# The squares of the second part's three norms summed on GpSimd, with one product with ones in place of eight

## The reference, cut to what matters

```python
def rmsnorm(x, gain):
    y = x * lax.rsqrt(jnp.mean(x * x, axis=-1, keepdims=True) + EPS)
    return y * gain

for i in range(2):
    h = rmsnorm(x, norm_mix[i])
    mix = s5_mixer(h, ...) if i % 2 == 0 else dsa_mixer(h, ...)
    x = x + mix
    x = x + swiglu(rmsnorm(x, norm_ffn[i]), w_gate_up[i], w_down[i])
```

## Time and profile before

| what | us |
|---|---|
| median of three executions | 3164.7 |
| the profiled execution, its own time | 3160.65 |
| its span, from first to last instruction | 3158.8 |
| busy: TensorE products | 2900.4 (92%) |
| busy: VectorE | 1864.0 (59%) |
| busy: ScalarE | 1393.9 (44%) |
| busy: GpSimd | 219.7 (7%), 167 instructions |

### The profile page before, as it was taken

The page is one execution under the profiler, slowest core; times in us unless marked ns, Lnnn a source line. Parts: engine busy times, 40 slices in busy tenths (PEclk is TensorE's granted clock), DMA queues, the critical chain, the costliest instruction groups (busy, mean ns, idle before and its releaser), DMA issues.

```text
span 3158.8 us, 35772 instructions
## 1 busy us (share of the span) xinstructions
PE 2900.4 (92%) x12800; PEld 2235.7 (71%) x12800; DVE 1864.0 (59%) x2206; ACT 1393.9 (44%) x1794; POOL 219.7 (7%) x167
## 2 busy tenths in 40 slices
PE   7999999985899999999993678999989999989998
PEld 2548878765677777777772566788867767768887
DVE  3435653564988888888887753333236685343322
ACT  2323233223667777777775323323223435333221
POOL 1100100003930000000001000000001100000000
PEclk9999999996999999999997879999999999999999
DMA  6921722314899989999993802222221110122221
GB/s 236 330 76 60 282 85 94 121 62 161 319 331 352 387 351 387 361 377 369 369 372 108 107 32 75 94 95 106 93 75 67 67 54 1 41 72 101 94 94 67
DMA packets 90801, 546.92 MB, mean 173 GB/s; under 512 B 9232, under 2 KB 18848, under 8 KB 32384
## 3 DMA queue, kind: packets, MB, share of 16 engines
q1 hardware_dynamic: 79584, 485.65, 41.6%
q0 software_dynamic: 10816, 59.58, 5.5%
q10 hardware_dynamic: 288, 0.15, 0.0%
HBM read 516.51 MB, written 41.42 MB: 177 GB/s over the span
## 4 chain that ended last, share of the span: by engine, by line
PE 69%; DVE 17%; issue 6%; DMA 4%; ACT 3%; SPq 1%; POOL 1%; DVEq 0%; ACTq 0%; PEldq 0%; POOLq 0%
PE bank L348 38%; PE bank L286 6%; PE bank L1138 5%; PE bank L1142 4%; PE bank L1141 4%; DVE expert_low L2218 4%; DMA arena<-in_we_stream 2%; ACT expert_high L1587 1%; PE bank L1370 1%; PE bank L1392 1%; PE bank L1383 1%; DMA arena<-in_mod 1%; PE bank L1122 1%; DVE expert_x_low L2303 1%; DVE arena L2320 1%
## 5 line engine op out<-in xcount | busy, mean ns | idle before, releaser
L2218 DVE TENSOR_TENSOR expert_low<-arena,expert_high 128x2048 fp32r<-128x2048 f32 x291 | 684.2, 2382 | 102.7 <-ACT expert_high L1587 85.4
L1587 ACT ACTIVATE expert_high<-arena 128x1024 fp32r<-128x1024 f32 x582 | 597.2, 1057 | 213.4 <-PE bank L1138 117.5
L348 PE MATMUL bank<-high_b,weight_parts 128*128 128x512 f32 x1872 | 592.9, 398 | 29.6 <-DVE low_b L2456 15.9
L716 DVE TENSOR_TENSOR weight_parts<-ring_pages,weight_parts 128x1024 fp32r<-128x1024 f32 x185 | 226.7, 1226 | 557.9 <-ACT weight_parts L708 557.4
L708 ACT ACTIVATE weight_parts<-ring_pages 128x1024 fp32r<-128x1024 f32 x185 | 196.1, 1060 | 591.6 <-PE bank L348 552.4
L348 PEld LDWEIGHTS bank<-high_b,weight_parts 128*128 128x128 f32 x1872 | 352.8, 190 | 121.1 <-issue 36.3
L348 PE MATMUL bank<-low_b,weight_parts 128*128 128x512 f32 x832 | 325.7, 391 | 0.0
L1138 PE MATMUL bank<-expert_high,expert_x_low 128*128 128x512 f32 x768 | 309.5, 403 | 14.1 <-DVE expert_low L2218 10.4
L1141 PE MATMUL bank<-expert_high,expert_x_high 128*128 128x512 f32 x768 | 301.1, 392 | 0.0
L1142 PE MATMUL bank<-expert_low,expert_x_high 128*128 128x512 f32 x768 | 300.6, 391 | 0.0
L348 PE MATMUL bank<-hidden_parts,weight_parts 128*128 128x512 f32 x1056 | 240.0, 389 | 4.3 <-DVE hidden_parts L2502 4.3
(11 more groups left out here) (464 smaller groups left out, 4033.2 us busy)
## 6 DMA issues: line engine op xcount, KB each, us to landing
arena<-in_we_stream SPq DMA_DIRECT2D x294, 1024.0 KB, 6.5
ring_pages<-in_wb_stream SPq DMA_DIRECT2D x93, 1024.0 KB, 4.8
ring_pages<-in_wa_stream SPq DMA_DIRECT2D x49, 1024.0 KB, 4.9
arena<-in_mod POOLq DMA_DIRECT2D x16, 1024.0 KB
xbuf<-arena POOLq DMA_DIRECT2D x25, 512.0 KB, 15.9
arena<-xbuf SPq DMA_DIRECT2D x17, 512.0 KB, 7.3
ybuf<-arena SPq DMA_DIRECT2D x16, 512.0 KB, 2.6
arena<-kd SPq DMA_DIRECT2D x8, 512.0 KB, 24.1
```

Source lines behind the costliest of these rows:

```text
L348: ins = pe.matmul(o, lhsT, rhs, start=start, stop=stop)
L716: nc.vector.tensor_tensor(low, src, high.bitcast(F32), ALU.subtract).then_inc(weights_split, 1)
L1587: nc.scalar.activation(ehigh[c % HIGH_E][:, at], ring_e[c % RING_E][:, at], ACT.Copy) \
L2218: nc.vector.tensor_tensor(elow[c % RING_E][:], ring_e[c % RING_E], ehigh[c % HIGH_E][:].bitcast(F32), ALU.subtract).then_inc(weights_split ...
```

## The change

GpSimd adds the eight squares of each norm into the first tile, with seven additions of 128x512 in place, each waiting for its square and for the addition before. It raises `sq_summed` by a separate instruction. TensorE waits for that one increment (the two of the first block make it count from 2) and multiplies the one summed tile by the ones. The sums of norms 2 and 3 stand in GpSimd's program behind the stores of the state-space matrices and ahead of the wait and the loads of the rotary tables. The sum of norm 4 stands behind the loop of the rotated tiles. Nothing else is changed.

```diff
@@ -909,6 +909,14 @@
+            def squares_summed(n):
+                for kt in range(1, KT):
+                    pool.wait_ge(S["b_sq_full"], KT * (n - 2) + kt + 1)
+                    link(nc.gpsimd.tensor_tensor(sqb[n][:, 0, :], sqb[n][:, 0, :], sqb[n][:, kt, :], ALU.add))
+                pool.sem_inc(S["sq_summed"], 1)
+
+            squares_summed(2)
+            squares_summed(3)
             pool.wait_ge(S["b_x_ready"], 2 * KT)
             for dst, src in ((cossin, io["cossin"]), (rope, io["rope"]), (half1, io["half1"])):
                 pool.dma_start(dst, src).then_inc(S["b_rope_in"], 16)
@@ -926,6 +934,7 @@
+            squares_summed(4)
         @block.tensor
@@ -1189,10 +1198,8 @@
             def squares(n):
                 ps = opened(f"sn{n}")
-                for kt in range(KT):
-                    pe.wait_ge(S["b_sq_full"], KT * (n - 2) + kt + 1)
-                    ins = pe.matmul(ps[:], ones[:], sqb[n][:, kt, :], start=(kt == 0), stop=(kt == KT - 1))
-                ins.then_inc(bank_done, 1)
+                pe.wait_ge(S["sq_summed"], n + 1)
+                pe.matmul(ps[:], ones[:], sqb[n][:, 0, :], start=True, stop=True).then_inc(bank_done, 1)
```

## The result

Over eleven executions of each, side by side on one chip, the changed kernel has a median of 3255.05 us (3172.36 to 3259.99) and the kernel before one of 3244.42 us (3161.42 to 3256.53). Taken on its lower end that is 11 us of loss, in the middle 17 us; I had forecast 9.5 us of loss and a time of 3171 us.

The account below looks back on a forecast made before the run. TensorE was taken to bound the kernel, waiting at the norms for the three roots. Roots later by 5.3, 2.1 and 2.1 us, together 9.5, on 3160.65 gave 3170.2; forecast 3171 us, range 3163 to 3183.

Parts of the forecast that it names:

- a median that lands on such a one: Whole kernel: the measured median falls on a disturbed execution like the one at 3247.57 us; chance 0.01.
- Squares in a burst, adding slower than squaring: Before each norm: squares start 0.52 us apart over about 5 us, GpSimd additions take 1.30 us each.
- Seven additions: GpSimd at each norm: seven chained additions of 1.30 us with 0.08 us between two, 9.58 us.
- The overlap with VectorE's last addition at norm 2: Norm 2: first GpSimd addition meets VectorE's last addition to x for 0.3 us, costing 0.0 to 0.5, taken as 0.
- Release by a separate increment: Each norm, GpSimd's last addition to TensorE: 0.29 us, ends 0.1 and 0.4.
- The product at the lower clock: TensorE's one product at each norm, after a gap above 6.56 us: 2.08 us, against 1.02 at full clock.
- The sum for a norm: First square's start to root's start: 13.20 us, roots 5.3, 2.1 and 2.1 us later at norms 2, 3, 4.
- What was costed at nothing: Later rotary table loads (cover 4 us), the low clock behind norms, ScalarE's table load, and VectorE overlap: 0 us.
- The ends of the range: Lower: full clock, shorter addition, plain release, 3164.7 us; upper: wider addition, overlaps, slower releases, the median's 4 us, 3182.9.
- additions keep up: Rival at the norms: additions keep pace with squares, only the last shows; norm 3 gains 2.8 us, total 3154; chance 0.04.
- The rival of a low clock: TensorE's clock stays low behind the norms' longer gaps, up to +220 us in an up projection, 3390; chance 0.01.
- The mutual hindrance of GpSimd and VectorE: Rival at the norms: additions take 3.36 us throughout, 43 us more, 3213; chance 0.02.

Follow-up runs that it names:

- early_sums: Changed kernel with a longer filler ahead of attention and ScalarE's squares of tiles 0 to 6 moved into the stage before; 3188.39 us, ratio 1.0077.
- experiment 5: Changed kernel with a longer filler ahead of attention, TensorE making 44 or 24 small products while waiting for the sum; 3201.88 us, one execution.
- after_again: Changed kernel timed once more with no edit and no added filler; 3178.26 us, ratio 1.0055.
- fill2_after: Changed kernel with longer filler ahead of the attention steps and more filler products further on in that stage; 3175.65 us, ratio 1.0045.
- fill2_before: Kernel before with longer filler ahead of the attention steps and more filler products further on in that stage; 3168.08 us, ratio 1.0018.

## Why the prediction was right or wrong

**The time was wrong.** The step that failed is the one in which I set 3247.57 aside as a disturbed execution and gave 0.01 to a median that lands on such a one. About half of the kernel's executions are at that level: the attention stage has two lengths by TensorE's clock, and what TensorE does in a wait of 1.52 us just ahead of it decides whether it takes the long one (with a longer filler there the highest cluster was empty in both kernels). The sum was put on 3160.65, an execution that had kept its clock; the measured median, 3255.05, is one that had not. Why the clock falls there in one execution and holds in the next is open. I had looked for what the clock does behind the norms and nowhere else; the profile before had happened to hold its clock, so nothing in it showed the cost, and only the three times did.

**The mechanism was right, and its size to 1 us** (8.6 of holes against 9.5). By its terms:

- Squares in a burst, adding slower than squaring: shown. Spreading them (early_sums) moved the holes from 31.1 to 16.5 us in all.
- Seven additions, 9.58 us forecast, 9.46, 9.37 and 9.38 measured: 1.26 us each, not 1.30, with pitches of 1.34. The scaled width (1.24) was the nearer row. The overlap with VectorE's last addition at norm 2, costed at 0.0 to 0.5, was 0.16: the first addition took 1.42.
- Release by a separate increment: 0.29 forecast, 0.19 us at norm 3 (2352.15 to 2352.34).
- The product at the lower clock: 2.08 forecast, 2.05 measured, 1.12 when TensorE was kept at work (experiment 5).
- The sum for a norm: 13.20 forecast, 12.97 at norm 2, 12.88 at norm 4 (2859.85 to 2872.73).
- What was costed at nothing held at the norms: the tables had landed in time, and root to next product stayed at 6.52 us, clock or no clock.
- The ends of the range: the terms gave 3164.7 at the lower one, and the range began at 3163 without a term for the rest; the wider addition is 3 x 0.78 = 2.3, not 2.5. Neither matters beside the 85 us.

**The loss measured as a ratio is larger than the holes:** 17 us against 8.6. Part of it is the executions between the clusters, of which the one profiled had its clock fall at the second place; without the two of the first eleven, the three left are 8 us above the median of the four lowest of before (3173.4 and 3165.3). With the clock held in both kernels it is 7.6 us. By the counts the change makes such a fall more likely (5 of the 15 that were not in the highest cluster, against 0 of 39); why it should, with stages that start 5 to 10 us later and the same instructions, is open. A further 1.6 us came behind a wait of 2.17 us between the up and the down projection, which both kernels have. Here the profile after, then that before:

```profile
2180.00:2260.00 80.00, 77.83 (x336) 63.90 (x336) 24.45 (x25) 19.95 (x23) 0.00 (x0) 0.98 0.26 92
```

```profile
2180.00:2260.00 80.00, 77.83 (x344) 64.13 (x343) 23.99 (x24) 18.83 (x21) 0.00 (x0) 1.00 0.26 92
```

Root 2 to root 3 is 383.65 us against 380.23, 1.6 more than the hole (383.64 in after_again). The second feed-forward block does the same: from root 4 to the end it is 383.5 us in both profiles of the changed kernel and 381.9 in that before. From norm 2 on, with the attention stage left out, the changed kernel is thus 8.6 + 1.6 + 1.5 = 11.7 us longer in these profiles, as much as lies between the lowest clusters (by how much the part ahead of norm 2 differs changes from profile to profile). These falls come and go and are not the change's alone: fill2_after has neither (382.08, the hole's 1.83 and no more, and 381.9), fill2_before has the second (383.5). What decides them is open.

**The rivals.** That additions keep up did not happen; with the squares spread it nearly does, and the 2.8 us at norm 3 that it promised became 1.8. The rival of a low clock had the right engine and the wrong place: not behind the norms, where it came back within the first groups, but in the stage of short products. The mutual hindrance of GpSimd and VectorE is there beside dense work (1.74 us) and absent in the holes, where VectorE is idle.

## What to carry to other kernels

Moving work off the bounding engine gains nothing where its consumers wait for the mover: compare the pace of the producer (0.52 us a square) with that of the new engine (1.34 us an addition), and look first whether the producer could be spread, since early squares with a two-step sum gained back the 8.6 us of holes that the change had lost, and 12.7 us more. When the few times of a kernel scatter by 3%, find out where before you forecast: a second profile of the slow kind showed it in one row of slices. In this kernel a stage of short products kept TensorE busy and at half clock for 100 us, and a few filler products ahead of it and in it moved the median of the executions more than any edit of the norms. Those ahead of it alone did only half the work: 17 of 19 executions then lay where a later fall in the stage puts them.

## What the runs showed of the hardware that was not expected

- TensorE stayed at PEclk 0.50 for over 120 us while it was busy in 100.00 of 100 us (331 instructions), with products of 64 to 128 columns for the most part. At 1.00 it runs 575 of them in 97.38 busy us. Both executions had the same wait of 1.52 us ahead of the stage; the clock fell behind it in one and not in the other.
- GpSimd's f32 addition of 128x512 took 1.26 us, its multiplication of the same size in the same program 1.30, and 1.74 where a two-input subtraction of VectorE overlapped it by 0.6 us.
